# Turned score products of the in-head rounds taken through the four column sets in turn, and the first gather of the ninth round placed in front of the eighth's

## What is computed

```python
N_HEADS, KV_LORA, QK_ROPE_DIM, V_HEAD_DIM = 8, 256, 64, 128
PAST_LEN, PAGE_SIZE, DEC_BATCH, DEC_SEQ = 4096, 128, 8, 4

def sample_attention(q_lat, q_pe, ckv_new, kpe_new, cache_ckv, cache_kpe, page_table):
    def one(args):
        ql, qp, cn, kn, pages = args
        cp = cache_ckv[pages].reshape(-1, KV_LORA)
        kp = cache_kpe[pages].reshape(-1, QK_ROPE_DIM)
        s_past = (einsum('thl,pl->htp', ql, cp) + einsum('thr,pr->htp', qp, kp)) * ATTN_SCALE
        s_new = ...                                   # causal, the 4 new tokens
        p = softmax(concatenate([s_past, s_new], axis=-1))
        return einsum('htp,pl->thl', p[..., :n_past], cp) + einsum('hts,sl->thl', p[..., n_past:], cn)
    return lax.map(one, ...)                          # over the 8 sequences
```

## Time and profile before

| | |
|---|---|
| median of 3 runs | 1348.68 us (1348.06 to 1358.08) |
| profiled execution | 1359.43 us, its span 1357.6 us |
| mean granted clock of TensorE in it | 0.991 |
| PE busy | 1325.6 us (98%), 11006 instructions |
| DVE, ACT, POOL busy | 786.1, 572.2, 688.2 us |
| DMA | 207.27 MB, mean 153 GB/s |

### The profile page before, as it was taken

One profiled execution on the slowest core, in us unless ns is written; L12 is line 12 of the kernel. 1 busy time (PEld: TensorE's weight loads), 2 busy tenths in 40 slices (PEclk: granted clock), 3 DMA queues, 4 the chain that ended last, 5 costly groups with the idle time before them and its releaser, 6 DMA issues.

```text
span 1357.6 us, 27728 instructions
## 1 busy us (share of the span) xinstructions
PE 1325.6 (98%) x11006; PEld 1235.7 (91%) x11006; DVE 786.1 (58%) x1198; ACT 572.2 (42%) x973; POOL 688.2 (51%) x467
## 2 busy tenths in 40 slices
PE   7999999999999999999999998899999999999998
PEld 7877599999999999999997776678999999999997
DVE  6688867554545453767545665565675454555534
ACT  5211455443434343535554443343464434343432
POOL 3322343587878785434441222121438888787831
PEclk9999999999999999999999998899999999999999
DMA  6654435676676334434256787872222323232321
GB/s 246 170 179 120 137 100 148 176 185 183 181 186 166 114 112 146 161 100 164 83 181 225 288 296 288 308 292 99 71 91 94 94 94 94 94 94 94 94 94 66
DMA packets 215569, 207.27 MB, mean 153 GB/s; under 512 B 110416, under 2 KB 196688, under 8 KB 207888
## 3 DMA queue, kind: packets, MB, share of 16 engines
q1 hardware_dynamic: 210448, 171.40, 41.3%
q0 software_dynamic: 4608, 33.56, 6.7%
q10 hardware_dynamic: 384, 0.55, 0.2%
HBM read 190.47 MB, written 31.42 MB: 163 GB/s over the span
## 4 chain that ended last, share of the span: by engine, by line
PE 94%; DMA 3%; ACT 1%; POOL 1%; issue 0%; DVE 0%; SPq 0%; DVEq 0%; ACTq 0%; POOLq 0%
PE ps L1906 34%; PE ps L2042 21%; PE ps L2030 19%; PE ps L1944 3%; PE ps L2236 2%; PE ps L2174 2%; PE ps L2283 2%; DMA nat<-cache_ckv,rows 2%; PE ps L2222 1%; PE ps L2378 1%; PE ps L1957 1%; PE ps L2107 1%; PE ps L2212 1%; DMA raw<-k_pages 1%; DMA kp<-k_pages 1%; PE ps L2133 1%
## 5 line engine op out<-in xcount | busy, mean ns | idle before, releaser
L709 POOL TENSOR_TENSOR wl<-raw,wh 128x512 fp32r<-128x512 f32 (+2 forms) x249 | 431.9, 1737 | 397.8 <-ACT wh L848 397.8
L848 ACT ACTIVATE wh<-raw 128x512 fp32r<-128x512 f32 (+2 forms) x253 | 192.3, 762 | 366.8 <-PE ps L1906 200.2
L1906 PE MATMUL ps<-xh,wh 128*128 128x272 f32 x704 | 148.5, 292 | 10.8 <-DVE xl L1254 9.9
L2042 PE MATMUL ps<-mh,wl 128*128 128x272 f32 x768 | 158.5, 288 | 0.0
L2042 PE MATMUL ps<-mh,wh 128*128 128x272 f32 x768 | 158.3, 287 | 0.0
L2042 PE MATMUL ps<-ml,wh 128*128 128x272 f32 x768 | 158.3, 288 | 0.0
L709 POOL TENSOR_TENSOR wl<-wuv,wh 128x512 fp32r<-128x512 f32 x104 | 133.8, 1297 | 47.7 <-ACT wh L848 47.7
L1906 PE MATMUL ps<-xl,wh 128*128 128x272 f32 x704 | 146.3, 289 | 0.0
L1906 PE MATMUL ps<-xh,wl 128*128 128x272 f32 x704 | 146.0, 289 | 0.0
L1906 PEld LDWEIGHTS ps<-xh,wh 128*128 128x128 f32 x704 | 111.5, 190 | 16.3 <-POOL wl L709 11.0
L2042 PEld LDWEIGHTS ps<-mh,wh 128*128 128x128 f32 x768 | 120.5, 188 | 0.0
(11 more groups left out here) (326 smaller groups left out, 2953.9 us busy)
## 6 DMA issues: line engine op xcount, KB each, us to landing
raw<-w_up SPq DMA_DIRECT2D x32, 1024.0 KB, 5.6
raw<-w_down SPq DMA_DIRECT2D x32, 1024.0 KB, 5.1
k_pages<-cache_kT SPq DMA_DIRECT2D x128, 160.0 KB, 3.4
raw<-k_pages SPq DMA_DIRECT2D x16, 1024.0 KB, 4.9
raw<-w_pw SPq DMA_DIRECT2D x11, 1024.0 KB, 5.5
kp<-k_pages SPq DMA_DIRECT2D x32, 256.0 KB, 5.3
shifted<-ext SPq DMA_DIRECT2D x96, 66.5 KB, 2.0
k_pages<-cache_kT SPq DMA_DIRECT2D x128, 32.0 KB, 2.2
```

The source lines that it names most:

```text
L709: pf.tensor_tensor(weight(wl, u), weight_raw(u), f32(weight(wh, u)), ALU.subtract).then_inc(w_lo, 1)
L848: af.activation(weight(wh, u), weight_raw(u), ACT.Copy).then_inc(w_hi, 1)
L1906: m = tf.matmul(ps[:, bank_of(u) + bank, 0:width], w[:, k, :], a[:, k, part], start=(k == 0 and n == 0), stop=(k == nk - 1 and n == 2))
L2042: m = tf.matmul(acc_of(u)[:, h, :], w[:, k, :], a[:, k0 + k, h * HALF:(h + 1) * HALF], start=(k0 == 0 and k == 0 and n == 0), stop=(k0 > 0 ...
```

## The change

Three places:

1. `turned_scores`: the loops over column set `s`, latent half `c` and parity `par` are turned inside out. Sets are now innermost, so that successive products go to sets 0, 1, 2, 3. Both key semaphores are waited for ahead of the first product, instead of the second one in the middle.
2. `gather(16)` moves from behind gathers 14 and 15 to ahead of their wait for the eighth round's keys.
3. `KEY_SLOT`: the rotary keys of chunks 16 and 17 (round 8) go into slots 0 and 1, and the cycle through the seven slots begins two chunks later.

```diff
-KEY_SLOT = [j % 2 if j < TURNED else (2, 3, 4, 5, 6, 0, 1)[(j - TURNED) % CB] for j in range(NCH)]
+KEY_SLOT = [j % 2 if j < TURNED + 2 else (2, 3, 4, 5, 6, 0, 1)[(j - TURNED - 2) % CB] for j in range(NCH)]
...
+                if h == NH - 1:
+                    pool.wait_ge(w_lo, UK[NH - 1] + 1)
+                    gather(TURNED)
                 if h > 1:
                     for k in range(2):
                         pool.wait_ge(t_keys[k], 16 * (h + 1))
                     gather(2 * h)
                     gather(2 * h + 1)
-            pool.wait_ge(w_lo, UK[NH - 1] + 1)
-            gather(TURNED)
             gather(TURNED + 1)
             gather(TURNED + 2)
...
-                for s in range(SETS):
-                    j = 2 * i + s // 2
-                    if s % 2 == 0:
-                        pe.wait_ge(t_keys[j % 2], 16 * (i + 1))
-                    for c in range(KC):
-                        for par in range(2):
+                for k in range(2):
+                    pe.wait_ge(t_keys[k], 16 * (i + 1))
+                for c in range(KC):
+                    for par in range(2):
+                        for s in range(SETS):
                             m = tf.matmul(scores_at(i, par)[NS * s:NS * (s + 1)].rearrange("p (q g s) -> p q g s", q=2, s=ROWS), qs[:, c, b, :],
-                                          page_order(turned_latents(j, par, c), s), start=False, stop=(c == KC - 1))
+                                          page_order(turned_latents(2 * i + s // 2, par, c), s), start=False, stop=(c == KC - 1))
```

## The result

| | before | after |
|---|---|---|
| median (runs) | 1350.87 us (8, 1348.06 to 1358.08) | 1340.87 us (8, 1339.53 to 1343.59) |
| ratio, 95% interval | | 0.991 (0.989 to 0.9931) |
| profiled execution, its span | 1359.43, 1357.6 us | 1340.17, 1338.4 us |
| mean granted clock in it | 0.991 | 0.993 |

The kernel became faster by 10.0 us, 0.9%. The forecast was 22 us (1327), its range 1315 to 1338; the time lies above the range. The forecast took its 22 us from 1348.7 us, the median of three runs; over eight runs the median of before is 1350.87.

What follows compares the result with a forecast made beforehand. PE, busy 98% of the span, was taken as the bound, with the DMA next in the heads. 10.0 (heads) + 12.1 (gap into the ninth round) - 0.5 = 21.6 us off 1348.7 gave 1327; range 1315 to 1338.

Steps and rivals of the forecast that it cites:

- behind: After the ninth round's values: gathers 19 and 20 move with the outputs and keep their lead; 0.5 us charged.
- the last one, from the profiled execution to the median: The whole 21.6 us, summed in the 1359.43 us execution, was taken off the 1348.7 us median, giving 1327.
- the heads: Up to the eighth scores' end: 823.0 instead of 833.0, a gain of 10.0 us, not 20.5.
- the gap: From the eighth scores' end to the ninth values' end: 27.1 us falls to 15.0, a gain of 12.1.
- Part 1, the batch: A head's 32 turned score products with sets in turn: 1.86 us instead of 4.5, saving 2.65 us per head.
- What is late next: In the heads, keys have 1.1 us of slack; then the DMA bounds them at a 15.5 us cycle, PE needing 13.7.
- Part 2: Gather 16 ahead shares the DMA with the last head's keys: 2.7 us later, PE standing 4.5 to 6 us.
- Part 3: Into the ninth round: no wait for gather 16 or rotary keys, gather 17 waited for 0.9 us; stretch 15.0 us.
- the 2.3 us charged for the clock in the last head: After PE's wait for the eighth round's keys the clock falls to the 1.2 GHz level, costing 2.3 us.
- The transfers eat more: Rival, chance 0.20: later keys, gather 17 or the unexplained 10.7 us leave a gain of 8 to 15 us, 1334 to 1341.
- The DMA keeps up: Rival, chance 0.15: no wait for keys in the heads, so a gain of 32.6 us, 1316.
- slower: Rival, chance 0.03: reading four page-ordered streams at once makes the sets serial in the heads' batches; 1359 us.

Runs made afterwards that it cites:

- the reference: The profile of the unchanged kernel that the prediction used, an execution of 1359.43 us.
- e1: The kernel before, run again with no edit: 1352.01 us, its profiled execution 1350.78 us.
- e5: The changed kernel with 512 KB per turned key transfer from the third chunk on, the samples' outputs wrong: 1330.42 us, ratio to before 0.9851.
- e8: The changed kernel with POOL's gathers in the heads waiting only for the first of the two turned keys: 1327.93 us, ratio to before 0.9822.
- e4: The changed kernel with gather 16 behind the wait for the eighth round's keys, still ahead of gathers 14 and 15: 1341.63 us, ratio to before 0.992.
- e7: The changed kernel with 28 unused products on PE to keep the clock up, around the last head and the ninth round: 1341.73 us, ratio to before 0.9925.
- e10: The changed kernel with POOL's gathers in the heads waiting for no turned key at all: 1342.19 us, ratio to before 0.9935.
- e9: The kernel before with 27 unused products on PE, in the last head and the ninth round's rotary scores: 1351.58 us, ratio 0.9999.

## Why the prediction was wrong, step by step

The terms of the sum, against both profiles of before (all from the times above; "behind" is from the ninth values' end to the span's end, where the reference has 497.52 us, e1 494.77 and after 494.84):

| | forecast | reference to after | e1 to after |
|---|---|---|---|
| up to the eighth scores' end | 10.0 | 833.17 - 825.61 = 7.6 | 831.36 - 825.61 = 5.8 |
| from there to the ninth values' end | 12.1 | 26.9 - 17.9 = 9.0 | 22.9 - 17.9 = 4.9 |
| behind | -0.5 | 2.7 | -0.1 |
| sum | 21.6 | 19.2 | 10.6 |

The first row holds what lies ahead of the heads too, where the kernels don't differ: the first rotary scores start at 711.85 in the reference, 710.53 in e1 and 712.05 in after. From there to the eighth scores' end it is 121.3, 120.8 and 113.6 us, so the heads gained 7.8 and 7.3, and the 5.8 of the table has 1.5 us of scatter in it.

**The step that failed first is the last one, from the profiled execution to the median.** The text took the whole 21.6 us from the median, 1348.7, as if the execution in which they were counted had been a typical one. It had named the other possibility, that the 10.7 us above the median are part of the waits that go, and priced it at 11 us and 1338; 10.0 and 1340.87 were measured. That this price came so near is in part luck. Of the 8.6 us between the two spans of before 4.0 lie in the very stretch that part 3 shortens and 0.5 in the heads, but 2.7 lie behind the ninth round and 1.3 ahead of the heads, which the change doesn't touch. The profile had a sign of it, in rows that the prediction used itself: the half clock of 840.30 to 844.90, at PE's longest wait. A single profile can't say how usual that is.

**The second is the size of two terms: 12.1 us for the gap and 10.0 for the heads.** Even in the reference they were 9.0 and 7.6, 5.5 us less together. Within its own trace the sum still came out only 2.4 us off (1338 there, 1340.17 measured), and that is luck: the 2.7 us behind the ninth round, charged at -0.5, made up for 3.2 of the 5.5. Against e1, the nearer to the median, the gap's term was 4.9, two fifths of the forecast. Of the 11.0 us between 21.6 and 10.6 (each rounded), 4.0 are the reference's longer gap, 2.9 after's gap (17.9 and not 15.0), 0.2 the rounded 27.1 for 26.9, 2.7 the heads and 1.5 the scatter ahead of them, less 0.4 behind.

**Part 1, the batch: right.** 1.86 us forecast, 1.93 with its tail; the first head's new wait for the softmax was 0.70 us, as worked out, and the third head's turned scores start 13.7 us behind the second's, the forecast pace of PE alone. In after the saving shows whole only in these first heads.

**What is late next: right in kind, short in size.** The keys became late, and the cycle is bound by full transfers plus the hole, as e5 and e8 show. The forecast cycle of 15.5 us was 15.9, 15.9 and 15.0. But the keys were further behind before it set in: those of head 2 took 10.2 us where 8.8 had been taken over from a head with no gathers in the way, those of head 3 took 12.6 and not 10.1. They landed at 756.43 and not 753.6, and everything behind kept that 2.6 to 2.8 us, up to the eighth scores' end at 825.6 and not 823.0. For head 3 the cause shows in the rows: its keys were asked for 3.5 us behind the first gather of head 2 (740.33, scores' end at 743.86), where before has 7.6 us between the two (743.23, 750.8), so the gathers were still moving. For head 2 it doesn't: no gather was in flight in after either (8 GB/s from 725.00 to 730.17), and why these keys took 1.3 us more stays open.

**Part 2: as worked out, and of little use.** Gather 16 is waited for no more, the eighth keys come 18.5 us behind the seventh (forecast 18.2), PE stands 3.2 and 1.8 us for them (forecast 4.5 to 6 in all) and goes on at half clock (2.93 us for the scores). But what gather 16 gains the next one loses: e4 has the same bytes in another order and a time that can't be told from after's.

**Part 3: 17.9 us instead of 15.0.** The rotary keys of round 8 are waited for no more, right. Gather 17 was named as next and put at 0.9 us at full clock; it was 1.42 us, and the 24 transposes behind it took 4.51 where e1's took 3.09. The outputs waited 1.03 instead of 0.6. That is 2.4 of the 2.9 us. That the half clock itself isn't the bound there shows in e7, where it went and the wait for gather 17 grew to 2.42 us. By the same run the 2.3 us charged for the clock in the last head were worth next to nothing. Gather 17 landed at 834.5 and not at 830.5, most of it because the eighth scores ended later; the "usual 0.7 us" in that part of the sum is shown by no row.

**The rivals.** "The transfers eat more", at 0.20, is the one that came, with 1334 to 1341 (1340.87 is at its edge), and with all three of its causes in part: later keys, gather 17 in gather 16's place, and the 10.7 us, of which 4.5 by e1 lay in what the change shortens. It deserved more than the forecast, since the last of them, by the prediction's own arithmetic, was enough alone. "The DMA keeps up" and "slower" are out; neither came near. The likeliest case and its range treated three causes that all point upward as a small remainder.

**Chances.** Faster by over 1% had 0.82. The ratio, 0.991, is within 1%, which had 0.15, though its interval (0.989 to 0.9931) reaches past 1%.

## What to carry to other kernels

Before a gain is taken off a median, the profiled execution has to be a typical one: if it is longer than the median by as much as the waits that the change removes, part of the saving may never have been in the median, and a second profile of the unchanged kernel is worth more than a finer sum. When PE's slack against the transfers is smaller than the saving, the saving buys only that slack until the order of the transfers changes too: here the change and one wait less on POOL together gave 24 us, the change alone 10 to 12, the wait alone nothing. When two transfers of one group are waited for before a third is issued, waiting for the first alone can shorten the hole and keep the order, as in e8; waiting for none gave the order away in e10 and only moved the hole.

## What the runs showed of the hardware

- The length of one wait alone didn't decide whether the granted clock fell. The wait for gather 16, in executions of one program, left it at 1.00 once (3.61 us, then 8 transposes in 1.09 us) and brought it to the 1.2 GHz level another time (4.16 us, then 1.97 us). It also fell behind a shorter wait of 3.04 us in e1 (scores in 2.88 us instead of 1.93) and behind one of 1.97 us in the reference. The Trainium skill, TensorE: Matmul & The Clock Gate, Part 1, says that activity releases the throttle and idleness brings it back, and these rows agree: each fall stands behind a wait.
- Of the 8.6 us between the two executions about 4.7 are work done at the lower clock (3.0 in the stretch, 1.7 behind it), 2.1 longer waits there, 1.3 scatter ahead of the heads and 0.5 the heads. That doesn't make the clock worth 4.7 us in a typical execution: keeping it at 1.00 (e9) narrowed the runs, from a standard deviation of 2.4 us to 1.1, and left the median where it was.
- Around the landing of the keys, up to the traffic of the gathers issued on it, the DMA engines move 56 GB/s (after) to 82 GB/s (before) over 4 us, against 394 in full stretches. Issuing the gathers one 1024 KB transfer earlier raised the mean of three heads from 312 to 333 GB/s.
- Thirty-two products of 128x32 by 256 columns with the column sets in turn start 55 ns apart (728.24 to 729.99 in after, 1.75 us), also where the moving operand is read in page order; one set after the other they start up to 213 ns apart.
